# Second pass's weight loads ahead of the constants, and a weight ring of their own for the down projections

## The reference

```python
x = x + 0.5 * swiglu(rmsnorm(x, ffn1_norm), w_gate, w_up, w_down)      # 1024 -> 2816 -> 1024
h = rmsnorm(x, mix_norm); p = h @ w_in                                  # 1024 -> 3072
att_out = diff_attention(q, k, v, ...)      # 4 heads, relative bias, first three 512 columns of p
hy_out  = hyena(z_hy, ...)                  # short conv, long conv by FFT with filters made by an MLP
x = x + concat([att_out, hy_out]) @ w_out
x = x + 0.5 * swiglu(rmsnorm(x, ffn2_norm), ...)
out = rmsnorm(x, final_norm)

def swiglu(x, w_gate, w_up, w_down):
    return (jax.nn.silu(x @ w_gate) * (x @ w_up)) @ w_down
```

## Time and profile before

| | us |
|---|---|
| median of 3 runs | 1075.18 (1073.84 to 1075.75) |
| profiled execution | 1077.74 |
| its span | 1075.9 |
| TensorE busy in it | 1040.3 (97%) |
| VectorE busy | 568.8 (53%) |
| ScalarE busy | 335.0 (31%) |
| HBM traffic over the span | 89 GB/s |

### The profile page before, as it was taken

The page is one execution under the profiler, slowest core; times in us unless marked ns, Lnnn a source line. Parts: engine busy times, 40 slices in busy tenths (PEclk is TensorE's granted clock), DMA queues, the critical chain, the costliest instruction groups (busy, mean ns, idle before and its releaser), DMA issues. The chain is left out here.

```text
span 1075.9 us, 12082 instructions
## 1 busy us (share of the span) xinstructions
PE 1040.3 (97%) x4551; PEld 824.4 (77%) x4551; DVE 568.8 (53%) x722; ACT 335.0 (31%) x477; POOL 60.9 (6%) x57
## 2 busy tenths in 40 slices
PE   9699999999999999999999969999999999999996
PEld 7577788888888876777775548778888888888885
DVE  5355644444433347866958495765454545433332
ACT  6222322323222242444434302432222222222222
POOL 0000000000000010000000061310000000000000
PEclk9899999999999998999999989999999999999999
DMA  7723233332333252323221000223333333332322
GB/s 165 205 80 97 79 97 97 96 99 85 96 93 108 88 178 73 95 59 95 61 78 59 1 20 19 79 85 94 101 91 98 96 97 97 93 107 89 93 69 78
DMA packets 184461, 96.69 MB, mean 90 GB/s; under 512 B 14812, under 2 KB 181860, under 8 KB 184425
## 3 DMA queue, kind: packets, MB, share of 16 engines
q1 hardware_dynamic: 183160, 92.70, 29.8%
q0 software_dynamic: 352, 1.85, 0.5%
q10 hardware_dynamic: 912, 1.64, 0.5%
HBM read 94.07 MB, written 2.11 MB: 89 GB/s over the span
## 5 line engine op out<-in xcount | busy, mean ns | idle before, releaser
L1130 PE MATMUL bank<-x_hi,w_hi 128*128 128x512 f32 x880 | 349.4, 397 | 12.4 <-DVE w_lo L707 12.0
L1131 PE MATMUL bank<-x_lo,w_hi 128*128 128x512 f32 x880 | 344.1, 391 | 0.0
L1132 PE MATMUL bank<-x_hi,w_lo 128*128 128x512 f32 x880 | 344.1, 391 | 0.0
L707 DVE TENSOR_TENSOR w_lo<-raw,w_hi 128x1024 fp32r<-128x1024 f32 x168 | 203.6, 1212 | 230.4 <-ACT w_hi L440 225.8
L440 ACT CAST w_hi<-raw 128x1024 fp32r<-128x1024 f32 x168 | 172.4, 1026 | 173.8 <-PE bank L1132 128.0
L1130 PEld LDWEIGHTS bank<-x_hi,w_hi 128*128 128x128 f32 x880 | 166.2, 189 | 59.9 <-issue 18.8
L1132 PEld LDWEIGHTS bank<-x_hi,w_lo 128*128 128x128 f32 x880 | 166.1, 189 | 35.3
L1131 PEld LDWEIGHTS bank<-x_lo,w_hi 128*128 128x128 f32 x880 | 166.4, 189 | 34.5 <-issue 1.0
L1130 PE MATMUL bank<-h_hi,w_hi 128*128 128x512 f32 x352 | 136.9, 389 | 0.0
L1131 PE MATMUL bank<-h_lo,w_hi 128*128 128x512 f32 x352 | 136.9, 389 | 0.0
L1132 PE MATMUL bank<-h_hi,w_lo 128*128 128x512 f32 x352 | 136.9, 389 | 0.0
(11 more groups left out here) (208 smaller groups left out, 782.4 us busy)
## 6 DMA issues: line engine op xcount, KB each, us to landing
raw<-in_ffn_w_gate SPq DMA_DIRECT2D x44, 512.0 KB, 3.8
raw<-in_ffn_w_up SPq DMA_DIRECT2D x44, 512.0 KB, 3.8
raw<-in_ffn_w_down SPq DMA_DIRECT2D x32, 512.0 KB, 3.6
raw<-in_w_in SPq DMA_DIRECT2D x24, 512.0 KB, 3.7
raw<-in_ffn_w_down SPq DMA_DIRECT2D x16, 384.0 KB, 3.1
raw<-in_w_out SPq DMA_DIRECT2D x8, 512.0 KB, 3.5
x_nat<-in_x SPq DMA_DIRECT2D x4, 512.0 KB, 7.1
out<-o_nat SPq DMA_DIRECT2D x8, 256.0 KB, 2.9
```

The lines of the kernel that those rows point to most:

```text
L707: nc.vector.tensor_tensor(w_lo[:, half, 0:kb, :], raw[:, slot, 0:kb, :], w_hi[:, half, 0:kb, :].bitcast(F32), ALU.subtract).then_inc(w_spl ...
L1130: nc.tensor.matmul(dst, w_hi[:, half, k, :], hi, start=first and k == 0, stop=False)
L1131: nc.tensor.matmul(dst, w_hi[:, half, k, :], lo, start=False, stop=False)
L1132: ins = nc.tensor.matmul(dst, w_lo[:, half, k, :], hi, start=False, stop=last and k == kb - 1)
```

## The change

Three edits.

1. In the first pass of SyncE's `gate_up`, the loads of tiles 4 to 7 (`body(1)`) are issued before `others`; the loop then begins with pass 2. In the second SwiGLU the order of loads stays, and only the loop is one pass shorter.
2. The four DFT tables leave `others`. The new `dft_tables` issues them after head 0's six weight loads, when tile 68 has been used.
3. Two new buffers `down_hi` and `down_lo`, of the size and depth of `w_hi` and `w_lo`, lie where the DFT tables are, and the tables' block has moved to the place just below h. `ring` chooses them for tiles 45 to 68 and 145 to 168 (the last number is not reached); all other tiles keep the old buffers. Semaphores and waits of the pipeline are unchanged.

```diff
@@ place ... @@
-        cos_t, _ = place("cos_t", [P, NT, FQ])
-        sin_t, _ = place("sin_t", [P, NT, FQ])
-        cos_i, _ = place("cos_i", [P, 2, S])
-        sin_i, _ = place("sin_i", [P, 2, S])
         act3, _ = place("act3", [FO, S])
         silu, silu_at = place("silu", [P, 2, S])
         mlp_u, tmp2_at = place("mlp_u", [FO, S])
         mlp_k, _ = place("mlp_k", [FO, S])
         _, vec_at = place("vec_room", [P, 2, S])
+        cos_t, tables_at = place("cos_t", [P, NT, FQ])
+        sin_t, _ = place("sin_t", [P, NT, FQ])
+        cos_i, _ = place("cos_i", [P, 2, S])
+        sin_i, _ = place("sin_i", [P, 2, S])
+        down_lo, _ = place("down_lo", [P, SPLIT, 8, P], F32R, at=tables_at)
+        down_hi, _ = place("down_hi", [P, SPLIT, 8, P], F32R, at=tables_at + 4 * SPLIT * 8 * P)
@@ new @@
+        def ring(n):
+
+            n = n if n < N_FF2 else n - N_FF2
+            return (down_hi, down_lo) if N_DOWN1 < n <= N_MIX else (w_hi, w_lo)
@@ SyncE @@
                 sp.dma_start(rel[:], a["rel_bias"]).then_inc(late_landed, 16)
                 sp.dma_start(onehot[:], a["c_onehot"]).then_inc(late_landed, 16)
+
+            def dft_tables():
+
+                sp.wait_ge(w_used, N_MIX + 1)
                 sp.dma_start(cos_t[:], a["c_cos"].rearrange("(t p) f -> p t f", p=P)).then_inc(dft_landed, 16)
...
                     load(g[:, :, P:2 * P], KD, 2)
                     load(u[:, :, P:2 * P], KD, 3)
+                    body(1)
                     others()
                 else:
                     body(0)
-                with sp.Fori(1, NF // 2) as i:
+                    body(1)
+                with sp.Fori(2, NF // 2) as i:
                     body(i)
...
                     load(w[:, :, m * D_ATT + h * P:m * D_ATT + (h + 1) * P], KD, N_MIX + 6 * h + m)
+                if h == 0:
+                    dft_tables()
@@ ScalarE, VectorE, TensorE @@
-                nc.scalar.copy(w_hi[:, half, 0:kb, :], raw[:, slot, 0:kb, :]).then_inc(w_hi_made, 1)
+                nc.scalar.copy(ring(n0)[0][:, half, 0:kb, :], raw[:, slot, 0:kb, :]).then_inc(w_hi_made, 1)
...
-                nc.vector.tensor_tensor(w_lo[:, half, 0:kb, :], raw[:, slot, 0:kb, :],
-                                        w_hi[:, half, 0:kb, :].bitcast(F32), ALU.subtract).then_inc(w_split, 1)
+                hi, lo = ring(n0)
+                nc.vector.tensor_tensor(lo[:, half, 0:kb, :], raw[:, slot, 0:kb, :],
+                                        hi[:, half, 0:kb, :].bitcast(F32), ALU.subtract).then_inc(w_split, 1)
...
+                hi_w, lo_w = ring(number(n0, stride, i) if isinstance(i, int) else n0)
...
-                    nc.tensor.matmul(dst, w_hi[:, half, k, :], hi, start=first and k == 0, stop=False)
-                    nc.tensor.matmul(dst, w_hi[:, half, k, :], lo, start=False, stop=False)
-                    ins = nc.tensor.matmul(dst, w_lo[:, half, k, :], hi, start=False, stop=last and k == kb - 1)
+                    nc.tensor.matmul(dst, hi_w[:, half, k, :], hi, start=first and k == 0, stop=False)
+                    nc.tensor.matmul(dst, hi_w[:, half, k, :], lo, start=False, stop=False)
+                    ins = nc.tensor.matmul(dst, lo_w[:, half, k, :], hi, start=False, stop=last and k == kb - 1)
```

## The result

The changed kernel takes 1065.0 us (median of 4 runs, 1064.76 to 1066.42) against 1075.2 (1073.84 to 1075.75): 10.2 us less, a ratio of 0.991 with a 95% interval of 0.9893 to 0.9927. The forecast was 1064.9.

A forecast was written before the change was run, and what follows sets the result against it. TensorE, busy 97% of 1075.9 us, was taken to bound the kernel, with time to win at tile 4. The parts summed 10.25 + 0 + 0, so 1075.18 − 10.25 = 1064.9 us, range 1062.8 to 1069.7.

The forecast's parts named there:

- The loss at tile 4: TensorE's wait and slow clock at tile 4 lose 10.79 us; 0.43 idle and 0.11 restart stay, 10.25 us won.
- What made tile 4 late: Tile 4's load was issued only at 32.26, behind constants and tables: order in SyncE's queue, not bandwidth or buffers.
- The sum: Terms for the three parts of the change added: 10.25 + 0 + 0 = 10.25 us, median 1064.9 us.
- The constants' readers: Constants now issued after tiles 4 to 7; filter MLP hidden by 4.4 us, tile 8 by 2.6 to 8: no cost.
- 2.44 from cast to TensorE: In gate_up, TensorE starts a weight tile 2.44 us after ScalarE's cast of it, the split between them included.
- slowest landing: Landing time of 9.4 us after issue, that behind the tables, used for the constants and tile 8's worse case.
- The tables in the mixer: Four tables issued after head 0's sixth weight load, 2.9 us of issues, 2.1 MB: cost 0 to 4.8 us, taken as 0.
- the rival: Tables hold up the filter product: `w4` lands 7.3 us later, 4.8 us lost, 1069.7 us; chance 0.09.
- the rival at tile 8: Wait moves to tile 8 behind the constants: 7.0 us plus 1.63 slow restart, 8.6 lost, 1073.5 us; chance 0.06.
- Sharing between queues: DMA engines take turns between queues, so tables on SyncE's queue would share with `w4` on ScalarE's; in full, 4.8 us.
- The new buffers: Down projections' weights in new buffers, 1032 matmuls: 0 us, plus or minus 1; a rival slows them, 1080.4 us, chance 0.05.

The follow-up runs named there:

- tables late only: Kernel before with one edit, the DFT tables issued in the mixer, constants still ahead of tile 4, old buffers kept: 1067.29 us against 1074.92, ratio 0.9935.
- 48 more: Changed kernel with 48 more small constant DMAs behind the constants, ahead of tile 8's load: 1094.24 us against 1073.57 for the kernel before, ratio 1.0188.
- order only: Kernel before with only the loads of tiles 4 to 7 issued ahead of all constants, tables early, old buffers: 1065.17 us against 1074.92, ratio 0.9916.
- tables beside `w4`: Changed kernel with old buffers, four or two DFT tables issued one weight load earlier: four 1077.85 us (ratio 1.0039), two 1072.44 us (0.9993) against the kernel before.

## Why the prediction was right

**The loss at tile 4.** Forecast: an idle of 0.43 and 0.11 of restart stay of 10.79, 10.25 us won. Measured: 35.19 − (34.53 + 0.227) = 0.43 idle. At the down projection the changed kernel is 272.77 − 262.21 = 10.56 us ahead. Of the 0.3 beyond the forecast, 0.22 had arisen before tile 4 (tile 3 ends at 34.53 instead of 34.75), in the loading of x, which the change doesn't touch.

**What made tile 4 late.** The prediction called the wait one of order "and not of bandwidth". That step was half wrong: 3.5 of the 9.4 us of landing were the tables' transfer, as tables late only shows. The sum didn't suffer, because the first edit gets tile 4 past both the issues and the bytes.

**The constants' readers.** All hidden, as forecast. The 48 more show that the cover is real and finite: the forecast's 2.44 from cast to TensorE was 2.45. The 9.4 us used as the slowest landing was no bound, though: with the tables early, tile 8 took 11.2. In the changed kernel it took 5.2, since the tables had left.

**The tables in the mixer.** Cost nothing that these runs can see in the changed kernel (order only, without them there, is within 1 us of it), as forecast, and the reason given, that they stand behind a weight load until `w4` is nearly in, is borne out by what moving them ahead of that load costs. Two sizes in it were off. The four issues took 388.31 to 394.33, 6.0 us and not 2.9; tile 74's load followed at 394.37, and since its slot's split ended only near 394.1, this cost it 0.3 us at most. And the rival was priced at 4.8 us. The 7.3 us of delay in it were right (7.1 to 9.6 measured), but the slow clock behind the wait, 3.8 to 5.6 us, was left out altogether, though the rival at tile 8 had been charged 1.63 us for a slow restart. The right price is 10 to 12.

**Sharing between queues.** Transfers on SyncE's queue delayed one on ScalarE's by 7.1 to 9.6 us for 2.1 MB and 3.3 to 5.8 for 1.05 MB, 3 to 6 us per MB. The Trainium skill ("DMA: Bandwidth & Descriptors", Queues, rings and completion order) says that the two queues have their rings on the same DMA engines, which take turns between them. The runs agree. The 8.1 us of rows 10, which the prediction took as a sign of it, show nothing by themselves: with no table ahead of it, `w4` took 5.6 to 8.1. In the changed kernel the sharing costs nothing that is seen, because of when the tables are issued.

**The new buffers.** 0 forecast, and no difference beyond 1 us measured. Whether there is one of some tenths stays open.

**The span.** It shrank by 11.3 and the median by 10.2. 0.64 us of it came at the start of the mixer (404.95 − 393.75 = 11.20 there, 10.56 before). It goes with ScalarE's issues of `decay_b` and `w4`, behind which the cast of tile 69 stands: 1.07 + 0.52 us against 1.27 + 1.11 in rows 10's kernel. Twelve profiles, all but those with tables beside `w4`, bear this out. Where the two issues take at most 1.75 us together, the filter product starts 131.5 us after the down projection; where they take more (1.90 to 2.38), it starts their sum and 129.8 us after it, so 132.18 in the kernel before. Kernels with old and with new buffers are in both groups, and so are profiles of the changed kernel itself. The issue times vary by themselves, and I don't count them to the change. That the median came out within 0.1 us of the forecast is luck: beside the experiments the same kernel was 9.1 and 8.0 us faster than the kernel before.

## What to carry to other kernels

Before a queue's order is blamed, split a late landing into issue and transfer: here either moving four loads ahead or taking 2.1 MB away from before them gave most of the same 10 us, and the gains don't add. A transfer that is moved must be judged at its new place by who lands next on any queue, and a wait that it causes must be priced with the slow clock behind it: 2.5 us of wait cost 6.5 to 8. Price a wait by the distance of starts and not by the idle time that is listed for it. When the loss is gone, read what is left of the same wait; reordering elementwise work of the same passes brought 4 us more.

## What the runs showed that I had not expected

- After a standstill of 2.55 us TensorE ran a product of 16 float32 matmuls at the 1.2 GHz level throughout, 14.02 us against 8.4 to 10.2. After one of 2.14 us, before tile 4 with the tables late only, it began at full rhythm and then ran eight matmuls at that level.
- Small column DMAs cost SyncE 0.78 to 0.86 us each when 24 to 48 follow one another, and 15.28 / 24 = 0.64 in the mixed row of the changed kernel. Issues get dearer behind bytes on their way: a weight load of 512 KB took 0.4 us behind the constants in the changed kernel, and 4.1 behind the tables with order only.
- The runs of one kernel on one chip differ with the mean granted clock: the changed kernel's spans on the last chip were 1062.0 us at 0.990 and 1067.5 at 0.985. A difference of 1 us between two medians of this kernel says nothing.
